# The attention stage of a hybrid decoder layer: another order in the vector engine's step, squares from SBUF, splits one per step, a negated minimum

## The chip, the cores and the metric

The kernel runs on one core of one Trainium2 chip. The metric is the device time of one execution in microseconds (us). The kernel before was run three times, with a median of 1177.88 us (1175.91 to 1178.47).

## The reference

One decoder layer on x (1024 tokens of width 1024), all in float32. What matters here is its differential attention: 4 heads, each with two score matrices from 64-wide queries and keys, one set of 128-wide values, causal, with a slope per head (ALiBi).

```python
def block(qb):
    sc = einsum('bhcqd,bhckd->bhcqk', q_blk, k) * scale          # scale = 64 ** -0.5, c = 0, 1
    bias = where(dist >= 0, -slopes[:, None, None] * dist, -inf)
    prob = softmax(sc + bias[None, :, None], axis=-1)
    att = prob[:, :, 0] - lam * prob[:, :, 1]
    return einsum('bhqk,bhkd->bhqd', att, v)
att = rms_norm(att, head_norm_w, HEAD_NORM_EPS) * (1.0 - lambda_init)
```

Around it stand, in order: RMSNorm and the input projection, a recurrent branch (RG-LRU), the output projection with its residual, and a mixture of 32 experts with a router.

## The kernel before

The program has three blocks, each ended by a barrier of all engines: `project_and_recur`, `attend` and the block that mixes, routes and runs the experts. Only `attend` is touched.

Names used below. TensorE is PE, VectorE is DVE, ScalarE is ACT, GpSimd is POOL and SyncE is SP, as in the profile. Each engine takes its own instructions in the order written, and semaphores order them across engines.

`attend` goes through 4 heads of 8 query tiles of 128 rows. Step s of a head takes the tile with the most keys first: tile s sees 8 - s blocks of 128 keys (`width[s]`), so the tiles become narrower through a head. `pipeline(emit)` runs 32 steps and 4 more that drain. In one step every engine works on several tiles, each a fixed number of steps behind (`behind(h, s, k)`):

- PE: scores of tile s (L687) into the two score buffers `ps_s`, the transposes of tile s-2 (L699) into `ps_t`, the product with the values of tile s-3 (L708) into one of two buffers `ps_o`.
- DVE: for each of the two score matrices, add the bias and keep the row maximum in one instruction (L642, L644, each with a read of its accumulator), then the negated and scaled maximum (L647). Then for tile s-1 the reciprocal of the row sums (L652), a coefficient (L654) and the combination of the two probabilities (L656). Last, for tile s-4, the scaling of the result in `ps_o` by the reciprocal row sum into `mixT` (L665).
- ACT: copy of the transposed tile s-2 (L589), the two exponentials of tile s with their row sums (L594), and for tile s-4 the squares of the result with their sum (L604), read from `ps_o` and scaled there.

Three hand-overs order this. The scores of a step wait for `scores_read`, counted after both DVE instructions of the step before, since there is one pair of score buffers. The exponentials wait for `max_ready`, counted by L647. The product L708 waits until `ps_o` is free, that is for `out_squared` of the tile two before it (s-5), counted by ACT's squares, which come after DVE's scaling of that tile (`out_scaled`).

Once per head the queries and keys of the next head are split into a high part (ACT, L581) and a rest (DVE, L629), one instruction of 128x1024 for each of q and k on each engine. ACT does both in step 2, ahead of the squares; DVE does both in step 4, ahead of L665. PE asks for them (`qk_split`) at the start of the next head, and after the last of them SP issues the load of `w_out` into `qkvT`.

The bias of a head is one tensor `bias8`, 128x1024. POOL multiplies it in place by a constant between two heads (L570), after the last scores of a head were read and before the first of the next.

Of the kernel before, what the change touches and what calls it, by code (L numbers as in the profile page):

```python
# [5 lines left out]
P = 128  # L6
F32 = mybir.dt.float32
# [12 lines left out]
DH = 128  # L20
# [464 lines left out]
def attend(nc, io, persist):  # L485
# [4 lines left out]
    with ExitStack() as ctx:  # L490
# [3 lines left out]
        v_nat = persist["v_nat"]  # L494
        bias8, lam_in = persist["bias8"], persist["lam_in"]
# [4 lines left out]
        row_max = sb("row_max", [P, TT, 2])  # L500
        neg_max = sb("neg_max", [P, TT, 2])
# [9 lines left out]
        lam_exp = sem("lam_exp")  # L511
        pool_own = sem("pool_own")
# [4 lines left out]
        max_ready = sem("max_ready")  # L517
        exp_done = sem("exp_done")
# [42 lines left out]
        @block.gpsimd  # L561
        def _(pool):

            with pool.Fori(1, HEADS) as h:

                pool.wait_ge(scores_read, h * TT + 1)
                pool.sem_inc(pool_own, 1)
                pool.tensor_scalar(bias8[:, :], bias8[:, :], 2.0 ** (-8.0 / HEADS), 1.0,  # L570
                                   ALU.mult, ALU.mult).then_inc(bias_ready, 1)

        @block.scalar
        def _(act):
# [3 lines left out]
            def split(h):  # L578

                for parts, row in ((q_parts, h), (k_parts, h + 4)):  # L580
                    act.activation(part_of(parts, h % 2, 0), tile(qkvT, row), ACT.Copy).then_inc(qk_high, 1)  # L581

            def emit(h, s):
                if at := behind(h, s, 2):
                    n, head, e = at
                    act.wait_ge(turned, n + 1)

                    act.wait_ge(pv_done, n + 1)
                    act.activation(attT[:, e % 2, 0:width[e]], ps_t[:, 0:width[e]], ACT.Copy).then_inc(turned_out, 1)  # L589
                if at := behind(h, s, 0):  # L590
                    n, head, e = at
                    act.wait_ge(max_ready, n + 1)
                    for c in range(2):
                        ins = act.activation(prob[:, e % 4, c, 0:width[e]], prob[:, e % 4, c, 0:width[e]], ACT.Exp,  # L594
                                             bias=neg_max[:, e, c:c + 1], scale=QK ** -0.5,
                                             accum_out=row_sum[:, e, c:c + 1])
                    ins.then_inc(exp_done, 1)
                if s == 2 and not last(h):
                    split(h + 1)
                if at := behind(h, s, 4):  # L600
                    n, head, e = at

                    act.wait_ge(out_scaled, n + 1)
                    act.activation(junk[:, e % 2], ps_o[e % 2][:, 0:DH], ACT.Square, scale=inv_sum[:, e, 0:1],  # L604
                                   accum_out=head_ss[:, span(head * TT + tile_of[e], 1)]).then_inc(out_squared, 1)


            act.sem_inc(qk_high, 2)
            pipeline(emit)

        @block.vector
        def _(dve):
            link = Link(dve, dve_own)
            dve.sem_inc(scores_read, 1)

# [9 lines left out]

            def split(h):
                dve.wait_ge(qk_high, h * 2 + 2)
                for parts, row in ((q_parts, h), (k_parts, h + 4)):
                    dve.tensor_tensor(part_of(parts, h % 2, 1), tile(qkvT, row),  # L629
                                      part_of(parts, h % 2, 0).bitcast(F32), ALU.subtract).then_inc(qk_split, 1)  # L630

            def emit(h, s):
                if at := behind(h, s, 0):
                    n, head, e = at
                    if s == 0:
                        dve.wait_ge(bias_ready, h + 1)

                    dve.wait_ge(scores_done, n + 1)

                    dve.sem_inc(dve_seen, 1)  # L640
                    b = bias8[:, SEQ - width[e]:SEQ]
# [4 lines left out]
                    dve.sem_inc(scores_read, 1)  # L646
# [12 lines left out]
                if s == 4 and not last(h):  # L659
                    split(h + 1)  # L660
                if at := behind(h, s, 4):
                    n, head, e = at
                    dve.wait_ge(pv_done, n + 3)
                    o = mixT[:, span(head + 4, 1), tile_of[e] * P:tile_of[e] * P + P]
                    dve.tensor_scalar(o.rearrange("p o n -> p (o n)"), ps_o[e % 2][:, 0:DH], inv_sum[:, e, 0:1], None,  # L665
                                      ALU.mult).then_inc(out_scaled, 1)

# [3 lines left out]
        def _(pe):  # L671
            for free, n in ((turned_out, 1), (pv_done, 2), (out_squared, 2)):
# [18 lines left out]
            def emit(h, s):  # L691
# [9 lines left out]
                if at := behind(h, s, 3):  # L701
# [3 lines left out]

                    pe.wait_ge(out_squared, n + 1)
                    for k in range(TT - e):
# [1188 lines left out]
```

## Time and profile before

| | us |
|---|---|
| median of 3 runs (lowest, highest) | 1177.88 (1175.91, 1178.47) |
| the profiled execution, its own time | 1176.9 |
| the span that its profile covers | 1174.8 |
| busy in the span: PE, DVE, ACT, POOL | 1056.3, 878.4, 729.8, 130.7 |
| mean granted clock of PE, share of full speed | 0.944 |
| `attend`, first bias addition to end of last scaling | 272.76 to 404.98 |

The profile shows one execution. "Busy" is the time in which an engine had an instruction in its datapath. For a matmul the end is modelled. The granted clock is what the throttle gave PE: 1.00 is 2.4 GHz and 0.50 is 1.2 GHz. A row of the timeline gives start, duration, engine, line, operation, output<-inputs and shape; in brackets stands how long the engine had been idle before it and whose work ended that. PEld is the load of PE's weights, DVEq the instruction queue of DVE (a semaphore step that is an instruction of its own).

### The profile page before, as it was taken

To read this page: it belongs to the slowest core of one execution; us is meant where nothing else is said; L and a number is where in the kernel's file an instruction comes from. 1 tells how busy PE (TensorE), PEld (TensorE's weight loads), DVE (VectorE), ACT (ScalarE), POOL (GpSimd) and SP (SyncE) were. 2 spreads that over 40 slices of the span, in tenths; PEclk is the share of its full clock that TensorE was granted. 3 is DMA by queue.
4 is the path that set the end of the run, shared out by engine and by line. 5 is a ranking of instruction groups with operands and counts; after the bars stand their busy time and mean duration, and the time that the engine had idled before them with its cause. 6 is when DMAs were issued, how large, how long until landed. Compare 5 with 4: busy or idle time off the path is not lost.

```text
span 1174.8 us, 15610 instructions
## 1 busy us (share of the span) xinstructions
PE 1056.3 (90%) x5171; PEld 870.6 (74%) x5171; DVE 878.4 (75%) x1287; ACT 729.8 (62%) x953; POOL 130.7 (11%) x162
## 2 busy tenths in 40 slices
PE   4899999997777799994999999999999999999950
PEld 3788777786565688883888888888888888888830
DVE  6311266505778777768799999999999999999977
ACT  6222465615656832223688888888888888888824
POOL 1000000000000100001021221221221211211110
PEclk7899999998889999995999999999999999999985
DMA  7111111100004164457599999999999999999577
GB/s 230 52 57 50 37 36 36 36 1 0 1 1 146 21 260 139 144 227 259 214 401 389 375 382 389 381 390 385 366 391 376 370 411 367 385 401 377 226 308 286
DMA packets 49526, 273.27 MB, mean 233 GB/s; under 512 B 12016, under 2 KB 22416, under 8 KB 37200
## 3 DMA queue, kind: packets, MB, share of 16 engines
q1 hardware_dynamic: 40144, 255.72, 55.6%
q0 software_dynamic: 9344, 17.06, 3.9%
q8 instruction: 21, 0.34, 0.1%
q14 instruction: 17, 0.14, 0.0%
HBM read 255.97 MB, written 33.55 MB: 246 GB/s over the span
## 4 chain that ended last, share of the span: by engine, by line
PE 59%; DVE 4%; DMA 1%; issue 0%; ACT 0%; SPq 0%; POOL 0%; POOLq 0%; DVEq 0%
PE ps_moe L68 18%; PE ps_moe L70 17%; PE ps_moe L72 17%; PE ps_moe L1382 2%; PE ps_moe L1184 1%; PE ps_moe L1406 1%; DVE qkvT L1777 1%; DVE gate_up L1754 1%; DVE w_lo L1347 1%; DMA y_d<-y_sb,y_entry 1%; DMA y_second<-y_d 1%; PE ps_moe L1174 1%; PE ps_moe L1167 0%; DVE wout_lo L977 0%; PE ps_moe L1234 0%
## 5 line engine op out<-in xcount | busy, mean ns | idle before, releaser
L1347 DVE TENSOR_TENSOR w_lo<-qkvT,w_hi 128x1024 fp32r<-128x1024 f32 x192 | 224.0, 1224 | 3.7 <-ACT w_hi L1343 1.2
L1343 ACT ACTIVATE w_hi<-qkvT 128x1024 fp32r<-128x1024 f32 x192 | 192.7, 1056 | 15.9 <-PE ps_moe L72 15.9
L68 PE MATMUL ps_moe<-w_hi,x_hi 128*128 128x512 f32 x512 | 162.6, 399 | 4.1 <-DVE x_lo L1391 4.1
L70 PE MATMUL ps_moe<-w_lo,x_hi 128*128 128x512 f32 x512 | 159.3, 392 | 0.0
L72 PE MATMUL ps_moe<-w_hi,x_lo 128*128 128x512 f32 x512 | 158.8, 391 | 0.0
L1347 DVE TENSOR_TENSOR w_lo<-gate_up,w_hi 128x1024 fp32r<-128x1024 f32 x128 | 148.1, 1224 | 2.3 <-ACT w_hi L1343 0.4
L1343 ACT ACTIVATE w_hi<-gate_up 128x1024 fp32r<-128x1024 f32 x128 | 126.4, 1056 | 4.9 <-PE ps_moe L72 4.9
L70 PEld LDWEIGHTS ps_moe<-w_lo,x_hi 128*128 128x128 f32 x512 | 96.9, 189 | 20.9
L72 PEld LDWEIGHTS ps_moe<-w_hi,x_lo 128*128 128x128 f32 x512 | 96.7, 189 | 21.0
L68 PEld LDWEIGHTS ps_moe<-w_hi,x_hi 128*128 128x128 f32 x512 | 94.7, 190 | 22.2 <-DVE x_lo L1391 4.5
L333 DVE TENSOR_TENSOR q_parts<-w_raw,k_parts 128x1024 fp32r<-128x1024 f32 x16 | 19.6, 1224 | 91.9 <-ACT k_parts L233 91.9
L68 PE MATMUL ps_moe<-w_hi,h_hi 128*128 128x512 f32 x256 | 82.8, 405 | 5.0 <-DVE h_lo L1415 5.0
L68 PE MATMUL ps_proj<-hT_hi,k_parts 128*128 128x512 f32 x256 | 81.5, 400 | 0.0
L70 PE MATMUL ps_moe<-w_lo,h_hi 128*128 128x512 f32 x256 | 79.8, 393 | 0.0
L70 PE MATMUL ps_proj<-hT_lo,k_parts 128*128 128x512 f32 x256 | 79.7, 393 | 0.0
L72 PE MATMUL ps_moe<-w_hi,h_lo 128*128 128x512 f32 x256 | 79.6, 392 | 0.0
L72 PE MATMUL ps_proj<-hT_hi,q_parts 128*128 128x512 f32 x256 | 79.6, 392 | 0.0
L1361 POOL COPY y_entry<-entries 128x1 int32 (+1 forms) x32 | 32.8, 1025 | 407.9 <-ACT y_sb L1419 407.9
L1347 DVE TENSOR_TENSOR w_lo<-down,w_hi 128x1024 fp32r<-128x1024 f32 x64 | 75.7, 1222 | 0.5
L1343 ACT ACTIVATE w_hi<-down 128x1024 fp32r<-128x1024 f32 x64 | 65.8, 1057 | 7.4 <-PE ps_moe L72 7.4
L1391 DVE TENSOR_TENSOR x_lo<-ps_moe,x_hi 128x1024 fp32r<-128x1024 f32 x32 | 39.2, 1225 | 34.4 <-ACT x_hi L1387 34.4
L1387 ACT ACTIVATE x_hi<-ps_moe 128x1024 fp32r<-128x1024 f32 x32 | 32.8, 1025 | 46.3 <-PE ps_moe L1382 46.3
(255 smaller groups left out, 1880.0 us busy)
## 6 DMA issues: line engine op xcount, KB each, us to landing
qkvT<-in_w_exp_gate SPq DMA_DIRECT2D x16, 2048.0 KB, 10.3
qkvT<-in_w_exp_up SPq DMA_DIRECT2D x16, 2048.0 KB, 15.2
gate_up<-in_w_exp_gate SPq DMA_DIRECT2D x16, 2048.0 KB, 10.6
gate_up<-in_w_exp_up SPq DMA_DIRECT2D x16, 2048.0 KB, 15.4
qkvT<-in_w_exp_down SPq DMA_DIRECT2D x16, 2048.0 KB, 14.5
down<-in_w_exp_down SPq DMA_DIRECT2D x16, 2048.0 KB, 14.7
w_raw<-in_w_in SPq DMA_DIRECT2D x10, 1024.0 KB, 5.2
hn_d<-qkvT SPq DMA_DIRECT2D x16, 512.0 KB, 3.8
```

The lines of the kernel that those rows point to most:

```text
L68: nc_mm(o, lh, rh[h], start=start, stop=False)
L70: nc_mm(o, lh, rl[h], start=False, stop=False)
L72: last = nc_mm(o, ll, rh[h], start=False, stop=stop)
L333: ins = dve.tensor_tensor(w_lo[:, c % 2], w_raw[:, c // 2, :, (c % 2) * P:(c % 2 + 1) * P], w_hi[:, c % 2].bitcast(F32), ALU.subtract)
L1174: mm = pe.transpose(ps_h[:, k // 4, (k % 4) * P:(k % 4 + 1) * P], x2_sb[:, n % 2, k * P:(k + 1) * P], ident[:, :])
L1184: mm = pe.matmul(ps_r[:, AT_LOGITS:AT_LOGITS + NG + NE], x2T[:, n % 2, k], w_rt[:, k], start=k == 0, stop=k == KT - 1)
L1343: act.activation(two(w_hi, r), raw_unit(u, par), ACT.Copy).then_inc(q.split_high, 1)
L1347: dve.tensor_tensor(two(w_lo, r), raw_unit(u, par), two(w_hi, r).bitcast(F32), ALU.subtract).then_inc(q.split_low, 1)
L1361: pool.tensor_copy(copy[:, par:par + 1], entries[:, span(chunk, 1)]).then_inc(ready, 1)
L1382: mm = pe.transpose(ps_t[:, k // 4, (k % 4) * P:(k % 4 + 1) * P], x_sb[:, par, k * P:(k + 1) * P], ident[:, :])
L1387: act.activation(x_hi[:, par], turned_rows(ps_t[:, :, :]), ACT.Copy).then_inc(q.x_high, 1)
L1391: dve.tensor_tensor(x_lo[:, par], turned_rows(ps_t[:, :, :]), x_hi[:, par].bitcast(F32), ALU.subtract).then_inc(q.x_ready, 1)
```

## The change

1. On DVE the scaling of tile s-4 (L665) is the first thing of step s instead of the last.
2. The buffer `ps_o` is free once that scaling is done: PE waits for `out_scaled`. ACT's squares read the scaled result from `mixT` in SBUF, without a scale.
3. The bias additions multiply by -(64 ** -0.5) and keep the minimum, directly into `neg_max`; `row_max`, L647 and `max_ready` go. Each of the two counts `scores_read` when it ends, and each exponential waits for its own of them. The exponential's scale becomes -1.
4. The split of the next head goes one matrix per step: ACT q in step 3 and k in step 4, behind the squares; DVE q in step 4 and k in step 5.
5. Every head has a bias of its own (`bias_more`, 12 KB more per partition). POOL computes the three new ones at the start of `attend`, one from the other, without waiting for scores.

```diff
+        bias_more = sb("bias_more", [P, HEADS - 1, SEQ])
+        bias = [persist["bias8"][:, :]] + [bias_more[:, n] for n in range(HEADS - 1)]
...
-            with pool.Fori(1, HEADS) as h:
-                pool.wait_ge(scores_read, h * TT + 1)
-                pool.sem_inc(pool_own, 1)
-                pool.tensor_scalar(bias8[:, :], bias8[:, :], 2.0 ** (-8.0 / HEADS), 1.0,
+            for h in range(1, HEADS):
+                pool.wait_ge(bias_ready, h)
+                pool.tensor_scalar(bias[h], bias[h - 1], 2.0 ** (-8.0 / HEADS), 1.0,
                                    ALU.mult, ALU.mult).then_inc(bias_ready, 1)
...   (ACT)
-                    act.wait_ge(max_ready, n + 1)
                     for c in range(2):
+                        act.wait_ge(scores_read, 2 * n + c + 3)
                         ins = act.activation(prob[:, e % 4, c, 0:width[e]], prob[:, e % 4, c, 0:width[e]], ACT.Exp,
-                                             bias=neg_max[:, e, c:c + 1], scale=QK ** -0.5,
+                                             bias=neg_max[:, e, c:c + 1], scale=-1.0,
                                              accum_out=row_sum[:, e, c:c + 1])
                     ins.then_inc(exp_done, 1)
-                if s == 2 and not last(h):
-                    split(h + 1)
...
-                    act.wait_ge(out_scaled, n + 1)
-                    act.activation(junk[:, e % 2], ps_o[e % 2][:, 0:DH], ACT.Square, scale=inv_sum[:, e, 0:1],
+                    act.wait_ge(out_scaled, n + 3)
+                    need(act, out_squared, n - 1)
+                    act.activation(junk[:, e % 2], mixT[:, head + 4, tile_of[e] * P:tile_of[e] * P + P], ACT.Square,
                                    accum_out=head_ss[:, span(head * TT + tile_of[e], 1)]).then_inc(out_squared, 1)
+                if s in (3, 4) and not last(h):
+                    split(h + 1, s - 3)
...   (DVE: L665 with its wait moved from the end of emit to its start, then)
-                    dve.tensor_tensor_reduce(prob[:, e % 4, 0, 0:width[e]], ps_s[0][:, 0:width[e]], b, 1.0, -3e38,
-                                             ALU.add, ALU.max, row_max[:, e, 0:1])
-                    link(dve.tensor_tensor_reduce(prob[:, e % 4, 1, 0:width[e]], ps_s[1][:, 0:width[e]], b, 1.0,
-                                                  -3e38, ALU.add, ALU.max, row_max[:, e, 1:2]))
-                    dve.sem_inc(scores_read, 1)
-                    dve.tensor_scalar(neg_max[:, e, :], row_max[:, e, :], -(QK ** -0.5), None,
-                                      ALU.mult).then_inc(max_ready, 1)
+                    for c in range(2):
+                        dve.tensor_tensor_reduce(prob[:, e % 4, c, 0:width[e]], ps_s[c][:, 0:width[e]], b, -(QK ** -0.5),
+                                                 3e38, ALU.add, ALU.min, neg_max[:, e, c:c + 1]).then_inc(scores_read, 1)
...
-                if s == 4 and not last(h):
-                    split(h + 1)
+                if s in (4, 5) and not last(h):
+                    split(h + 1, s - 4)
...   (PE)
-                pe.wait_ge(scores_read, h * TT + (s + 1))
+                pe.wait_ge(scores_read, 2 * (h * TT + s) + 2)
...
-                    pe.wait_ge(out_squared, n + 1)
+                    pe.wait_ge(out_scaled, n + 1)
```

## Rows read from the trace of the kernel before

**Rows 1.** Chain that ended last, its earliest piece that does work (start, us).
```profile
405.75 0.63 ACT c_hi L898
```

**Rows 2.** Windows, by head: length, busy PE, PEld, DVE, ACT, POOL, clock, DMA share, GB/s.
```profile
272.76:305.90 33.14, 25.17 (x167) 20.49 (x168) 24.88 (x67) 20.39 (x48) 1.05 (x1) 0.79 0.00 1
305.90:341.46 35.56, 27.50 (x182) 22.76 (x180) 26.53 (x75) 22.09 (x56) 1.04 (x1) 0.81 0.00 1
341.46:373.75 32.29, 23.22 (x182) 18.37 (x181) 26.49 (x74) 23.12 (x60) 1.04 (x1) 1.00 0.23 78
373.75:404.98 31.23, 25.95 (x183) 20.84 (x181) 25.64 (x79) 22.90 (x64) 0.00 (x0) 0.89 0.14 57
```

**Rows 3.** Waits in 270 to 406: who waited for whom, total us, times, longest.
```profile
DVE prob L642 <- PE ps_s L687: 18.5, 18, 2.7
PE ps_o L708 <- ACT junk L604: 17.4, 15, 2.4
```

**Rows 4.** Windows, one per step of head 2 (steps 0 to 7), cut at L642's starts.
```profile
341.46:345.64 4.18, 2.81 (x21) 1.95 (x19) 3.45 (x10) 2.18 (x6) 0.00 (x0) 1.00 0.00 0
345.64:349.89 4.25, 2.19 (x18) 1.64 (x18) 4.03 (x10) 3.22 (x8) 0.00 (x0) 1.00 0.00 0
349.89:353.73 3.84, 2.69 (x23) 2.12 (x24) 3.62 (x11) 3.40 (x8) 0.00 (x0) 1.00 0.00 0
353.73:359.52 5.79, 3.98 (x31) 3.24 (x32) 3.30 (x11) 5.30 (x13) 0.00 (x0) 1.00 0.00 0
359.52:364.84 5.32, 3.66 (x31) 2.99 (x29) 5.10 (x11) 2.33 (x5) 0.00 (x0) 1.00 0.01 3
364.84:367.88 3.04, 2.32 (x20) 2.10 (x21) 2.50 (x11) 2.65 (x9) 0.00 (x0) 1.00 0.51 131
367.88:370.22 2.34, 2.34 (x22) 1.97 (x21) 2.11 (x9) 1.86 (x7) 0.00 (x0) 1.00 0.94 278
370.22:373.75 3.53, 3.23 (x25) 2.36 (x24) 2.37 (x9) 2.18 (x9) 1.04 (x1) 1.00 1.02 413
```

**Rows 5.** Timeline of head 2, step 0: from the last bias addition on.
```profile
343.75 0.08 DVE L644 DVE_READ_ACCUMULATOR2_ANT row_max<- 128x1 f32 x1
343.95 1.50 PE L687 MATMUL ps_s<-k_parts,q_parts 64*128 64x512 f32 x12 [0.97 <-DVEq L646]
344.06 0.16 DVE L652 RECIPROCAL inv_sum<-row_sum 128x2 f32<-128x2 f32 x1
344.51 0.35 DVE L656 SCALAR_TENSOR_TENSOR prob<-prob,coef 128x128 f32<-128x128 f32 x1
```

**Rows 6.** Timeline, step 3 of heads 1 and 2: first product with the values.
```profile
322.08 2.02 PE L708 MATMUL ps_o<-qkvT,attT 128*128 128x128 f32 x16 [2.26 <-ACT junk L604]
356.41 2.02 PE L708 MATMUL ps_o<-qkvT,attT 128*128 128x128 f32 x16 [1.81 <-ACT junk L604]
```

**Rows 7.** Timeline, steps 4 and 5 of heads 0 to 2.
```profile
296.16 2.77 PE L708 MATMUL ps_o<-qkvT,attT 128*128 128x128 f32 x12 [2.35 <-ACT junk L604]
331.23 2.90 PE L708 MATMUL ps_o<-qkvT,attT 128*128 128x128 f32 x12 [2.35 <-ACT junk L604]
...
363.44 1.22 DVE L629 TENSOR_TENSOR k_parts<-qkvT,k_parts 128x1024 fp32r<-128x1024 f32 x1
364.58 0.34 DVE L665 TENSOR_SCALAR mixT<-ps_o,inv_sum 128x128 f32<-128x128 f32 x1
```

**Rows 8.** Windows of head 1, steps 1 and 5.
```profile
310.10:315.10 5.00, 3.74 (x18) 2.89 (x18) 4.11 (x9) 3.92 (x11) 0.00 (x0) 0.50 0.00 0
330.51:335.26 4.75, 4.03 (x19) 3.61 (x20) 2.50 (x10) 2.81 (x9) 0.00 (x0) 0.50 0.00 0
```

**Rows 9.** Timeline, step 7 of head 0: POOL's bias and DVE beside it.
```profile
303.05 1.05 POOL L570 TENSOR_SCALAR bias<-bias 128x1024 f32<-128x1024 f32 x1 [67.75 <-DVEq L646]
303.22 0.88 DVE L654 SCALAR_TENSOR_TENSOR coef<-row_sum,lam,inv_sum 128x1 f32<-128x1 f32 x1
```

**Rows 10.** Groups of instructions in 270 to 406, the first bias addition.
```profile
L642 DVE CUSTOM_DVE_ANT_0 prob<-ps_s,bias 128x1024 f32<-128x1024 f32 (+7 forms) x32 | 24.2, 756 | 20.6 <-PE ps_s L687 18.5 <-issue 2.0
```

More of the change, by code:

```diff
@@ L494, in attend @@
         v_nat = persist["v_nat"]
-        bias8, lam_in = persist["bias8"], persist["lam_in"]
+        bias_more = sb("bias_more", [P, HEADS - 1, SEQ])
+        bias = [persist["bias8"][:, :]] + [bias_more[:, n] for n in range(HEADS - 1)]
+        lam_in = persist["lam_in"]
         prob = sb("prob", [P, 4, 2, SEQ])
@@ L499, in attend @@
         lam = sb("lam", [P, 8])
-        row_max = sb("row_max", [P, TT, 2])
         neg_max = sb("neg_max", [P, TT, 2])
@@ L511, in attend @@
         lam_exp = sem("lam_exp")
-        pool_own = sem("pool_own")
         qk_high = sem("qk_high")
@@ L516, in attend @@
         scores_read = sem("scores_read")
-        max_ready = sem("max_ready")
         exp_done = sem("exp_done")
@@ L576, in _, with split @@
             act.activation(lam[:, 2:4], lam[:, 0:2], ACT.Exp).then_inc(lam_exp, 1)
-            def split(h):
-                for parts, row in ((q_parts, h), (k_parts, h + 4)):
-                    act.activation(part_of(parts, h % 2, 0), tile(qkvT, row), ACT.Copy).then_inc(qk_high, 1)
+            def split(h, side):
+                parts, row = ((q_parts, h), (k_parts, h + 4))[side]
+                act.activation(part_of(parts, h % 2, 0), tile(qkvT, row), ACT.Copy).then_inc(qk_high, 1)
             def emit(h, s):
@@ L613, in _ @@
             link = Link(dve, dve_own)
-            dve.sem_inc(scores_read, 1)
+            dve.sem_inc(scores_read, 2)
             dve.sem_inc(qk_split, 2)
@@ L624, in _, with split @@
             link(dve.tensor_scalar(lam[:, 5:6], lam[:, 4:5], -LAM_INIT, None, ALU.add))
[L626 to L630, printed above, removed]
-            def emit(h, s):
+            def split(h, side):
+                parts, row = ((q_parts, h), (k_parts, h + 4))[side]
+                dve.wait_ge(qk_high, h * 2 + side + 1)
+                dve.tensor_tensor(part_of(parts, h % 2, 1), tile(qkvT, row),
+                                  part_of(parts, h % 2, 0).bitcast(F32), ALU.subtract).then_inc(qk_split, 1)
+            def emit(h, s):
+                if at := behind(h, s, 4):
+                    n, head, e = at
+                    dve.wait_ge(pv_done, n + 3)
+                    o = mixT[:, span(head + 4, 1), tile_of[e] * P:tile_of[e] * P + P]
+                    dve.tensor_scalar(o.rearrange("p o n -> p (o n)"), ps_o[e % 2][:, 0:DH], inv_sum[:, e, 0:1], None,
+                                      ALU.mult).then_inc(out_scaled, 1)
                 if at := behind(h, s, 0):
@@ L640, in emit @@
                     dve.sem_inc(dve_seen, 1)
-                    b = bias8[:, SEQ - width[e]:SEQ]
-                    dve.tensor_tensor_reduce(prob[:, e % 4, 0, 0:width[e]], ps_s[0][:, 0:width[e]], b, 1.0, -3e38,
-                                             ALU.add, ALU.max, row_max[:, e, 0:1])
-                    link(dve.tensor_tensor_reduce(prob[:, e % 4, 1, 0:width[e]], ps_s[1][:, 0:width[e]], b, 1.0,
-                                                  -3e38, ALU.add, ALU.max, row_max[:, e, 1:2]))
-                    dve.sem_inc(scores_read, 1)
-                    dve.tensor_scalar(neg_max[:, e, :], row_max[:, e, :], -(QK ** -0.5), None,
-                                      ALU.mult).then_inc(max_ready, 1)
+                    b = bias[head][:, SEQ - width[e]:SEQ]
+                    for c in range(2):
+                        dve.tensor_tensor_reduce(prob[:, e % 4, c, 0:width[e]], ps_s[c][:, 0:width[e]], b, -(QK ** -0.5),
+                                                 3e38, ALU.add, ALU.min, neg_max[:, e, c:c + 1]).then_inc(scores_read, 1)
                 if at := behind(h, s, 1):
@@ L658, in emit @@
                                              op0=ALU.mult, op1=ALU.add).then_inc(att_ready, 1)
-                if s == 4 and not last(h):
-                    split(h + 1)
[L661 to L666, printed above, removed]
+                if s in (4, 5) and not last(h):
+                    split(h + 1, s - 4)
             pipeline(emit)
@@ L671, in _ @@
         def _(pe):
-            for free, n in ((turned_out, 1), (pv_done, 2), (out_squared, 2)):
+            for free, n in ((turned_out, 1), (pv_done, 2), (out_scaled, 2)):
                 pe.sem_inc(free, n)
```

## The prediction

> **What bounds the kernel now.** Three views were read, in this order: the chain of waits for where the end is decided, the windows by head and step for who is busy, and the list of waits with the timeline for what each idle stretch waits for. The chain begins with ACT's first work of the last block, at 405.75 us [rows 1]: it cannot be followed through the barrier that ends `attend`. What comes behind is one unbroken chain, so every us by which `attend` ends earlier comes off the end. `attend` itself must be read by its waits.
>
> The four heads take 33.1, 35.6, 32.3 and 31.2 us, and in none is an engine busy throughout: DVE is busy 25 to 27 us, PE 23 to 28, ACT 20 to 23 [rows 2]. So the stage is bound by hand-overs. Head 2, which ran wholly at full clock, shows where: DVE is busy for 4.03 of 4.25 us in step 1 and 3.62 of 3.84 in step 2, so DVE bounds those; in step 3 it is busy for 3.30 of 5.79, in step 4 DVE for 5.10 of 5.32 while PE has 3.66 [rows 4]. The list of waits names the two large ones: DVE waits 18.5 us for scores, PE waits 17.4 us before its product with the values for ACT's squares [rows 3]. They are one wait: PE's queue holds the next scores behind that product.
>
> **The change part by part.**
>
> *The buffer is freed by DVE's scaling, which is first in its step (edits 1 and 2).* In step 3 PE stood still before the first product of heads 1 and 2 for 2.26 and 1.81 us, until ACT's squares ended [rows 6]; ACT had put two splits of a later head ahead of them. The scaling it will wait for is then over a step old. PE goes from transposes to product at once, the scores follow directly, and the interval shrinks by the idle time: -2.26 and -1.81. What is late next is PE itself: 3.98 us busy in that step [rows 4]. For head 3 the same wait was short (I take 0.4, from PE's place in the step), and head 0 had no earlier tiles in step 3. Does the scaling, now ahead of the bias addition, hold it up? It waits for the product of tile s-4, and PE does that before the scores of step s, for which the bias addition waits anyway. A scaling takes 0.34 us [rows 7] and lies beside those scores. Where DVE is bound it costs what it cost at the end of the step. Only the drain gains more: its last three products no longer wait for squares, some 0.3 us less each from the duration of scaling plus squares; I take -0.7 for the drain.
>
> The squares read SBUF. ACT has 9 us idle in every head [rows 2] for eight of them, so each would have to grow by over 1 us to matter: between -0.1 and +0.1 us each, hidden, counted 0. The trace has no square from SBUF; the Trainium skill (ScalarE: Activation LUTs, "The pipeline for one element") says that ScalarE lies closer to PSUM, which speaks against this edit; by it the squares get a little dearer, and the sum stays.
>
> *The split goes one per step (edit 4).* Step 4 holds both of DVE's splits; each takes 1.14 us of its queue (362.31 or so to 363.44 to 364.58) ahead of the scaling [rows 7]. That scaling, and then the squares, are what PE waits 2.35 us for in step 5 of heads 0, 1 and 2 [rows 7]. With one split moved out and the negation gone (below) step 4 becomes 5.32 - 1.14 - 0.23 = 3.95, still DVE's: -1.37 in each of three heads. Step 5 gets the other split: DVE's 2.50 busy [rows 4] less 0.17 for the negation plus 1.14, 3.5 with its gaps, against 3.04 in head 2 (+0.5). In head 1 the step took 4.75 us, because PE began its product late and at half clock, after the idle time [rows 8]; there it is -1.2, and in head 0, whose product took 2.77 instead of about 1.6 [rows 7], about -1.1. ACT's splits, 1.0 us each, stand in steps 3 and 4 behind the squares. Step 3 had 5.30 us of ACT, which includes two splits [rows 4]; with one and without the squares' place in line it has about 4.0 in a step of 4.0, so ACT is close to a bound there. DVE needs q one step later, which leaves about 1.4 us; if ACT slips by more, each us is lost once per head. The load of `w_out`, which SP issues after head 3's last split, moves by under 1 us against its head's start; it was in by step 0 of head 3 (the DMA columns of [rows 2, 4]), a head before it is read.
>
> *Negated minimum (edit 3).* From the end of the last accumulator read (343.83) to L652 are 0.23 us, in which L647 stood; then 0.45 to L656 [rows 5]. The 0.23 goes wherever DVE is the bound: steps 1, 2 of heads 1 to 3 and, counted above, step 4. PE started its scores 0.12 us after that read, through a queue instruction; a count by the instruction itself should take about 0.05, so -0.07 in step 0, where the ring "both additions, scores, both additions" bounds (4.18 us with DVE busy only 3.45 [rows 4]). The exponentials start some 1.5 us earlier, but nobody waited for them: 0 now, slack for ACT above. Steps 6 and 7 together go from 5.87 to about 5.24 in head 2: the additions of tile 6 (0.78), to L656 (0.45), that combination (0.62), the transposes and product behind it (1.5), scores of the next head (1.7) and hand-overs (0.2). That is -0.63, about -0.6 in head 0 and -1.0 in head 1 (low clock).
>
> Does the addition with another scale and a minimum cost more? The trace has only one form, 756 ns in the mean, 32 of them and as many beside it [rows 10]. I take the same: it is one pass over the row either way. The bounds are -0 and, if it took a second pass, twice that; the far end is a rival below.
>
> *A bias per head (edit 5).* Three POOL instructions of 1.05 us move from the head boundaries to the start. At the boundary DVE's coefficient L654 took 0.88 instead of 0.22 us beside L570 [rows 9]; PE had more to do in that step, so nothing is gained. At the start they meet four tiny DVE instructions and perhaps the first bias addition, which had 0.7 us to spare. Bounds: 0, and 3 x 1.05 less 0.7, 2.4. I take +0.4, since a row shows 0.66 for one such meeting and only the last matters. The Trainium skill (SBUF - State Buffer, "Who interferes with whom") has the rule: a DVE instruction with two SBUF inputs and a GpSimd one that reads SBUF exclude each other, while DVE with one SBUF input is not touched. L654 agrees (0.88 us); by it the first bias addition, with one input in PSUM, is not held, and the cost is between 0 and 0.4.
>
> **The sum** against the profiled execution's 1176.9 us, which is 1.0 below the median:
>
> | | removed, us |
> |---|---|
> | head 0 | 1.37 + 1.1 + 0.6 + 0.2 = 3.3 |
> | head 1 | 0.1 + 0.2 + 2.26 + 1.37 + 1.2 + 1.0 = 6.1 |
> | head 2 | 0.07 + 0.2 + 0.2 + 1.81 + 1.37 - 0.5 + 0.63 = 3.8 |
> | head 3 | 0.3 + 0.4 + 0.4 + 0.7 = 1.8 |
> | start | -0.4 |
>
> Together 14.6, so 1162.3: 1162 us. The heads would take about 29.9, 29.4, 28.5 and 29.4 us.
>
> **The rivals.**
>
> *A. PE's clock keeps or takes back part of it.* Heads 0 and 1 ran at 0.79 and 0.81, head 2 at 1.00 [rows 2], and half clock followed PE's idle time: step 5 of head 1 at 0.50 stands behind the 2.35 us [rows 7, 8], step 1 at 0.50 behind the ring of step 0. My sum lets the first kind go, since its idle time goes. For that: the gap is gone. Against: step 1 of head 1 fell without a gap over 2 us. If they stay, heads 0 and 1 lose 1.1, 1.2 and 0.4 + 0.3 again: 1165. If head 2 also gets two such spells (head 1 was 3.3 us longer in all): 1168. The other way round, if the ring's spells vanish too (5.00 against 4.25 in heads 1 and 3, 0.8 each), 1160. The Trainium skill (TensorE: Matmul & The Clock Gate, Part 1) says that the low level is the default and activity lifts it; a fuller PE should then have fewer spells, which is the 1160 end. The trace fits, head 1 apart.
>
> *B. DVE's order is the bound after all.* DVE is busy for 26 us a head; if every gap removed on PE is filled by DVE waiting elsewhere (ACT's slip above, splits arriving late in steps 4 and 5), the two stalls give half: 14.6 less half of 2.26 + 1.81 + 3 x 1.37 + 2.3, 9.4: 1168. For it: steps 1, 2 and 4 are DVE's already. Against: step 3, where the largest stall is, has 2.5 us of DVE idle.
>
> *C. Slower: the new form of the bias addition.* It is on the ring and in DVE's own bound in every step. Its 64 instructions take 48.4 us, twice 24.2 [rows 10]. From +0.23 us each, 30% more, it eats the 14.6; at a second pass the time is 1162 + 48 = 1210. Against it: the addition, the comparison and the multiplication are one instruction already, with a scale of 1.0.
>
> **How the numbers follow.** Forecast, 1158 to 1166: 0.70. A or B beyond it, to 1170: 0.17. More than forecast, below 1158 (the exponentials' head start or a shorter ring give more): 0.08. C or another cost that turns the sign: 0.03. No difference: 0.02. Faster is 0.95, within 0.2% (about 2.4 us, what a measurement of this kernel can tell) 0.02, slower 0.03. The range runs from 1156 to 1168: it takes in A's 1165 and the edge of its 1168, and the start's bounds.
>
> **What would show it.** L708 of step 3 no longer behind ACT's line, with under 0.5 us idle ahead of it; the same in step 5; L647 gone and L652 within 0.1 us of the accumulator read; steps 4 and 5 of heads 0 to 2 near 4.0 and 3.5 us; three L570 in a row near 270 to 274; mean clock of heads 0 and 1 over 0.85. The prediction is wrong if PE's wait before L708 is replaced by one for L589 (ACT), if DVE waits for `qk_high`, if L642 is slower than 756 ns in the mean, or if the heads stay over 31 us.

## The result, and the profile after

The changed kernel takes 1158.62 us in the median of four runs (1158.39 to 1158.93), the one before 1177.81; 19.2 us less. The ratio is 0.9846 (95% interval 0.9832 to 0.9861), which is 16 to 20 us less. Forecast were 1162 and a range of 1156 to 1168.

The profiled execution took 1158.54 us with a span of 1156.7. The last block now begins at 385.67 us instead of 405.73 [rows 1]; behind it lie 771.0 us instead of 769.1. That difference is not the change's: over the profiled executions of the experiments below this part took 768.1 to 771.7 us without relation to the edits. Nor is it the change's that `attend` began 0.55 us earlier, for DVE's first instruction in it did too (269.87 against 270.45 us). `attend` itself, from the first bias addition to the end of the last scaling, fell from 132.22 to 112.75 us: 19.5 us.

The windows by head of the kernel after (stretch, length, busy time of PE, PEld, DVE, ACT, POOL, granted clock, DMA share, GB/s) answer to [rows 2]; the last one ends with the last scaling:

```profile
272.21:301.80 29.59, 23.32 (x167) 19.07 (x168) 23.21 (x60) 19.95 (x48) 0.72 (x1) 0.83 0.01 1
301.80:329.57 27.77, 23.25 (x182) 19.36 (x181) 24.62 (x66) 21.57 (x58) 0.00 (x0) 0.94 0.00 1
329.57:357.72 28.15, 23.38 (x182) 19.42 (x181) 24.55 (x66) 21.60 (x58) 0.00 (x0) 0.94 0.12 34
357.72:384.96 27.24, 22.07 (x183) 18.56 (x181) 24.16 (x70) 21.52 (x64) 0.00 (x0) 1.00 0.31 124
```

The heads became 3.6, 7.8, 4.1 and 4.0 us shorter. DVE's busy time fell by only 1.5 to 1.9 us a head; the rest is idle time that went. DVE is now busy for 87 to 89% of heads 1 to 3, so it is nearly the bound.

The windows by step of head 2 answer to [rows 4]:

```profile
329.57:333.70 4.13, 2.56 (x22) 1.98 (x21) 3.29 (x9) 3.07 (x7) 0.00 (x0) 1.00 0.00 0
333.70:338.08 4.38, 2.73 (x18) 2.08 (x17) 3.95 (x8) 2.74 (x7) 0.00 (x0) 0.78 0.00 0
338.08:341.62 3.54, 3.27 (x23) 2.82 (x23) 3.47 (x8) 1.82 (x3) 0.00 (x0) 0.79 0.01 2
341.62:345.36 3.74, 3.74 (x31) 3.21 (x32) 3.15 (x9) 3.74 (x12) 0.00 (x0) 1.00 0.00 0
345.36:349.24 3.88, 3.88 (x36) 3.51 (x35) 3.81 (x10) 3.88 (x12) 0.00 (x0) 1.00 0.02 6
349.24:352.70 3.46, 2.93 (x27) 2.53 (x26) 3.39 (x10) 3.38 (x9) 0.00 (x0) 1.00 0.00 0
352.70:354.63 1.93, 1.19 (x12) 0.86 (x11) 1.86 (x9) 1.43 (x7) 0.00 (x0) 1.00 0.14 38
354.63:357.72 3.09, 3.09 (x25) 2.43 (x26) 1.64 (x9) 1.55 (x7) 0.00 (x0) 1.00 0.97 275
```

Read the length against each engine's busy time: in step 0 none fills it (the ring of additions and scores, 4.13), in steps 2, 4, 5 and 6 DVE does but for 0.07 us, in steps 3 and 7 PE does. In step 4 PE and ACT are full as well. Step 1 holds a spell at half clock (0.78 in the mean) and is 4.38 us long with DVE busy for 3.95.

The waits between 270 and 388 us answer to [rows 3]. The row for PE's product behind ACT's squares is gone, and that product waits for nothing else; what is left in the main is PE waiting for DVE's additions and DVE for PE's scores, the two sides of the ring:

```profile
PE ps_s L682 <- DVE neg_max L648: 16.6, 13, 2.8
DVE prob L648 <- PE ps_s L682: 13.3, 17, 2.8
ACT junk L601 <- DVE mixT L636: 0.3, 1, 0.3
```

In the timeline of head 2 the first product of step 3 has no idle time in brackets, against 1.81 us [rows 6], the one of step 5 starts at 348.79, 0.45 us before its step begins, and one split stands in each of two steps [rows 7]:

```profile
342.33 1.95 PE L703 MATMUL ps_o<-qkvT,attT 128*128 128x128 f32 x16
...
347.84 1.22 DVE L628 TENSOR_TENSOR q_parts<-qkvT,q_parts 128x1024 fp32r<-128x1024 f32 x1
...
348.79 1.50 PE L703 MATMUL ps_o<-qkvT,attT 128*128 128x128 f32 x12
...
348.98 0.34 DVE L636 TENSOR_SCALAR mixT<-ps_o,inv_sum 128x128 f32<-128x128 f32 x1
...
350.19 0.08 DVE L648 DVE_READ_ACCUMULATOR2_ANT neg_max<- 128x1 f32 x1
350.19 0.16 DVE L653 RECIPROCAL inv_sum<-row_sum 128x2 f32<-128x2 f32 x1
...
351.31 1.22 DVE L628 TENSOR_TENSOR k_parts<-qkvT,k_parts 128x1024 fp32r<-128x1024 f32 x1
```

### The profile page after: what moved, and what is told of

Read it like the earlier page. It is cut to its first block, busy times and chain, and to the rows that moved or that the text cites. A ratio compares the mean times of both kernels' runs of the same rounds, so it can differ in the third digit from the quotient of the medians.

```text
span 1156.7 us, 15563 instructions
## 1 busy us (share of the span) xinstructions
PE 1049.0 (91%) x5171; PEld 866.5 (75%) x5171; DVE 872.4 (75%) x1255; ACT 726.7 (63%) x953; POOL 130.5 (11%) x162
## 4 chain that ended last, share of the span: by engine, by line
PE 60%; DVE 4%; DMA 1%; issue 1%; ACT 0%; SPq 0%; POOL 0%; POOLq 0%; DVEq 0%
PE ps_moe L68 18%; PE ps_moe L70 18%; PE ps_moe L72 18%; PE ps_moe L1377 2%; PE ps_moe L1179 1%; PE ps_moe L1401 1%; DVE qkvT L1772 1%; DVE gate_up L1749 1%; DMA y_d<-y_sb,y_entry 1%; DVE w_lo L1342 1%; DMA y_second<-y_d 1%; PE ps_moe L1169 1%; PE ps_moe L1162 0%; DVE wout_lo L972 0%; PE ps_moe L1229 0%
## 5 line engine op out<-in xcount | busy, mean ns | idle before, releaser
L1382 ACT ACTIVATE x_hi<-ps_moe 128x1024 fp32r<-128x1024 f32 x32 | 32.8, 1026 | 46.2 <-PE ps_moe L1377 46.2
```

The source lines that it names most:

```text
L1382: act.activation(x_hi[:, par], turned_rows(ps_t[:, :, :]), ACT.Copy).then_inc(q.x_high, 1)
```

## The experiments

Each is timed in five rounds, beside runs of the kernel before, whose median was 1176.4 to 1178.4 us. The last block alone differs by up to 3.6 us from one profile to the next, so a second measure stands beside the medians: the length of `attend` itself in the one profiled execution of each run, first bias addition to end of last scaling.

| run | median, us | `attend`, us |
|---|---|---|
| kernel before | 1177.8 | 132.22 |
| before, edit 2 alone | 1165.5 | 118.57 |
| before, edit 4 alone | 1168.9 | 123.81 |
| before, edits 2 and 4 | 1163.6 | 118.18 |
| changed kernel | 1158.6 | 112.75 |
| changed, edit 4 undone | 1160.2 | 115.90 |
| changed, PE waits for the squares | 1160.4 | 113.38 |
| changed, edit 1 undone | 1158.8 | 113.42 |
| changed, edit 3 undone | 1162.9 | 118.00 |
| changed, edit 5 undone | 1158.0 | 112.38 |
| changed, scores of step 1 by matrix | 1152.6 | 107.95 |
| changed, product ahead of transposes | 1158.7 | 115.13 |
| changed, DVE's other order | 1155.8 | 110.16 |
| changed, both of the improvements | 1150.2 | 103.98 |

"Theory S" is the prediction's: two stalls of PE, both behind squares that stand behind splits, and DVE's own work for the rest.

### One part alone, on the kernel before

**Edit 2 alone.** PE takes the buffer after the scaling; ACT's squares read `mixT`, as in the change (not repeated here); nothing else.

```diff
-            for free, n in ((turned_out, 1), (pv_done, 2), (out_squared, 2)):
+            for free, n in ((turned_out, 1), (pv_done, 2), (out_scaled, 2)):
...
-                    pe.wait_ge(out_squared, n + 1)
+                    pe.wait_ge(out_scaled, n + 1)
```

> The kernel before with edit 2 alone: PE takes the values' buffer when the scaling is done, the squares read the scaled result; the order, both splits in one step and the separate negation stay. Theory S (two stalls, both PE waiting for squares that stand behind splits): the 2.26, 1.81 and 0.4 us ahead of the first product in step 3 go; the 2.35 us in step 5 shrink only by a square (0.5), because the scaling itself stands behind both DVE splits; the drain gives 1. Together 6 to 7 us less, 1171. Rival F (freeing by the scaling is nearly the whole change): 1162 or less. Rival O (DVE's work alone sets the time, waits are hidden): no difference.

Measured: 1165.49 us (1161.13 to 1167.38), ratio 0.9899 (0.9883 to 0.9916), 11.6 us less. The mechanism is S's, the size is not. Steps 3 to 5 of head 2, as windows:

```profile
346.94:350.67 3.73, 3.73 (x31) 3.20 (x32) 3.29 (x11) 3.73 (x8) 0.00 (x0) 1.00 0.00 0
350.67:355.99 5.32, 3.66 (x31) 2.98 (x29) 5.10 (x11) 3.57 (x11) 0.00 (x0) 1.00 0.00 2
355.99:358.62 2.63, 2.25 (x19) 1.95 (x20) 2.41 (x10) 2.24 (x7) 0.00 (x0) 1.00 0.38 97
```

Step 3 lost its stall (5.79 to 3.73), step 4 with both DVE splits is still 5.32 [rows 4]. In step 5 the product still waits 1.85 us, now for the scaling behind the splits. What S left out is the clock: steps 1 and 5 of head 1, at 0.50 before [rows 8], take 4.24 and 2.63 us here, against 4.25 and 2.63 in head 2.

S also left out a third group of waits, in step 1. Before the change the product of step 1 waited 1.26, 1.35 and 1.36 us for squares in heads 1 to 3, which is 4.0 of the 17.4 us of [rows 3]; behind it PE fell to half clock in heads 1 and 3. With edit 2 alone this wait is gone, and step 1 runs at full clock in heads 1 to 3. It isn't that PE idles less: in steps 0 and 1 of head 1 together it now stands still for 1.64 and 1.71 us around its scores, before for 1.63 and 1.26. Step 1 of head 1, first before and then with edit 2:

```profile
311.49 1.19 PE L708 MATMUL ps_o<-qkvT,attT 128*128 128x128 f32 x4 [1.26 <-ACT junk L604]
312.62 2.29 PE L687 MATMUL ps_s<-k_parts,q_parts 64*128 64x512 f32 x12
```

```profile
309.42 0.61 PE L709 MATMUL ps_o<-qkvT,attT 128*128 128x128 f32 x4
311.74 1.31 PE L688 MATMUL ps_s<-k_parts,q_parts 64*128 64x512 f32 x12 [1.71 <-DVEq L647]
```

**Edit 4 alone.** One split per step, behind the squares.

```diff
-                if s == 2 and not last(h):
-                    split(h + 1)
...   (behind the squares)
+                if s in (3, 4) and not last(h):
+                    split(h + 1, s - 3)
...   (DVE)
-                if s == 4 and not last(h):
-                    split(h + 1)
+                if s in (4, 5) and not last(h):
+                    split(h + 1, s - 4)
```

> The kernel before with edit 4 alone: ACT splits q in step 3 and k in step 4 behind the squares, DVE q in step 4 and k in step 5. Theory S: the squares of step 2 are no longer behind two splits, so step 3 loses its stall (4 to 4.5 us in all); step 4 loses 1.14 three times, step 5 gains 1.14 of DVE but loses most of the 2.35 us wait. Together 8 to 10 us less, 1169. Rival F: under 3 us less, because PE still waits for squares. Rival O: no difference.

Measured: 1168.86 us, ratio 0.9932 (0.9919 to 0.9945), 8.3 us less, where S had it. Steps 1 and 3 to 5 of head 1:

```profile
306.94:311.95 5.01, 3.68 (x19) 2.90 (x18) 4.12 (x10) 3.92 (x11) 0.00 (x0) 0.55 0.01 3
...
315.80:320.14 4.34, 3.97 (x31) 3.23 (x32) 3.30 (x10) 4.32 (x12) 0.00 (x0) 1.00 0.00 0
320.14:324.32 4.18, 3.67 (x31) 2.99 (x29) 3.96 (x10) 2.94 (x6) 0.00 (x0) 1.00 0.00 0
324.32:328.09 3.77, 2.71 (x22) 2.25 (x22) 3.55 (x11) 3.19 (x8) 0.00 (x0) 1.00 0.00 0
```

Steps 3, 4 and 5 fell from 6.24, 5.32 and 4.75. Step 5 runs at full clock; the idle time in it is about half of the 2.35 us before:

```profile
325.04 1.58 PE L708 MATMUL ps_o<-qkvT,attT 128*128 128x128 f32 x12 [1.21 <-ACT junk L602]
```

In step 1, where the wait for squares stays (1.33 us in head 1), PE fell to half clock as before. It still waited 12.8 us in all for squares.

**Edits 2 and 4 together**, both diffs above.

> The kernel before with edits 2 and 4 together. Alone they took 11.6 and 8.3 us. Theory S, as it stands after those runs: both remove the same stall (PE behind squares behind splits), and once the scaling frees the buffer DVE's two splits only move work between steps 4 and 5 (7.95 us together in the run with edit 2 alone, 4.2 + 3.8 with both): 1164 to 1166, no gain over edit 2 alone. Rival P (the splits' place has a gain of its own): 1160 or less.

Measured: 1163.60 us (1161.45 to 1165.25), ratio 0.9892 (0.9877 to 0.9908). Alone they took 11.6 and 8.3 us, together 12.8 (13.7, 8.4 and 14.0 in `attend`): for the most part they remove the same stall. Steps 4 and 5 of head 2 are 7.95 us together, exactly as with edit 2 alone (5.32 + 2.63):

```profile
347.12:351.30 4.18, 3.65 (x31) 2.98 (x29) 3.96 (x10) 3.28 (x8) 0.00 (x0) 1.00 0.03 6
351.30:355.07 3.77, 2.78 (x22) 2.25 (x22) 3.55 (x11) 3.13 (x8) 0.00 (x0) 1.00 0.00 0
```

### One part undone, on the kernel after

**Both splits in one step again** (edit 4 reversed).

```diff
-                if s in (4, 5) and not last(h):
-                    split(h + 1, s - 4)
+                if s == 4 and not last(h):
+                    split(h + 1)
```

and on ACT likewise, back into step 2 ahead of the squares.

> The changed kernel with edit 4 undone: both splits in one step again, ACT's in step 2 ahead of the squares, DVE's in step 4. Theory S: with the scaling first nobody waits for the squares, so DVE's two splits only move work between steps 4 and 5, whose sum is DVE's either way (7.3 us a head): 1 to 3 us over the changed kernel, 1160 to 1162. Rival P (the placement of the splits is the gain whatever frees the buffer): 6 us or more over it, 1165.

Measured: 1160.21 us (1158.32 to 1166.32), ratio 0.9865 (0.9843 to 0.9887). The medians put it 1.6 us over the changed kernel and `attend` 3.2; rival P's 1165 lies just beyond the interval. Steps 4 and 5 of head 1:

```profile
317.88:323.15 5.27, 5.13 (x43) 4.58 (x43) 5.03 (x11) 4.72 (x14) 0.00 (x0) 1.00 0.00 0
323.15:325.48 2.33, 0.74 (x7) 0.54 (x8) 2.26 (x9) 1.60 (x6) 0.00 (x0) 1.00 0.00 0
```

PE did 5.13 us of work in step 4 and 0.74 in step 5 (3.66 and 4.03 before): it runs ahead while DVE splits, and catches nothing up later. The sum, 7.60, is DVE's either way (7.34 after the change). Head 2 did worse in this profile: its step 6 held a spell at half clock and took 3.93 us, against 2.32 in head 1.

**PE waits for the squares again** (the hand-over of edit 2 reversed; the squares still read `mixT`).

```diff
                     pe.wait_ge(out_scaled, n + 1)
+                    pe.wait_ge(out_squared, n + 1)
```

> The changed kernel with PE waiting for the squares again before it takes the values' buffer (they still read the scaled result). Theory S: with the splits behind the squares and the exponentials 1.2 us earlier, ACT has the squares done within 0.3 us of when PE asks; 0 to 2 us over the changed kernel, 1159 to 1161. Rival F: the stalls come back, 6 us or more over it, 1165.

Measured: 1160.36 us, ratio 0.9855 (0.9841 to 0.9869). Rival F falls: with edits 1, 3 and 4 in place the squares are done when PE asks. PE's whole wait for them is this row of its list of waits:

```profile
PE ps_o L704 <- ACT junk L601: 0.5, 2, 0.3
```

So in the changed kernel the hand-over of edit 2 is worth little more. That doesn't make edit 4 its equal: alone on the kernel before it left 12.8 us of waits for squares. What brought them from 12.8 to 0.5 must lie in the other edits, above all edit 1 (the scaling first) or edit 3 (exponentials earlier); neither was undone in this kernel, so which one it is stays open.

**The scaling last in DVE's step** (edit 1 reversed: the block with L636 stands behind the splits).

```diff
-                if at := behind(h, s, 4):      (L636, first in emit)
...
+                if at := behind(h, s, 4):      (L636, last in emit)
```

> The changed kernel with edit 1 undone: DVE scales tile s-4 last in step s again. Theory S: PE then waits for a scaling behind a split in step 5, up to 0.5 us a head, and where scores are the bound the 0.26 us was hidden anyway: 0 to 2 us over the changed kernel, 1159 to 1161. Rival Q (the order is what frees PE early): 4 us or more over it.

Measured: 1158.81 us, ratio 0.9843 (0.9829 to 0.9856): no difference from the changed kernel. The order of edit 1 is worth nothing measurable as long as the scaling frees the buffer; PE waited 3.8 us in all for scalings, the longest 0.75 in step 6.

**Maximum and negation back** (edit 3 reversed).

```diff
-                    for c in range(2):
-                        dve.tensor_tensor_reduce(..., b, -(QK ** -0.5), 3e38, ALU.add, ALU.min,
-                                                 neg_max[:, e, c:c + 1]).then_inc(scores_read, 1)
+                    (two additions with 1.0, -3e38, ALU.max into row_max, the second waited for)
+                    dve.sem_inc(scores_read, 1)
+                    dve.tensor_scalar(neg_max[:, e, :], row_max[:, e, :], -(QK ** -0.5), None,
+                                      ALU.mult).then_inc(max_ready, 1)
```

> The changed kernel with edit 3 undone: maximum, then a separate negation (L647 of the kernel before), one count for both additions, exponentials behind the negation. Theory D (DVE is now the bound in 6 of 8 steps, and each pays the 0.23 us between the last accumulator read and the reciprocal): 32 x 0.23 less the ring's steps, 5 to 7 us over the changed kernel, 1164 to 1166. Rival H (hidden, as PE's queue decides): under 2 us.

Measured: 1162.92 us, ratio 0.9886 (0.9871 to 0.9902), 4.3 us over the changed kernel by the medians and 5.3 by `attend`: at the lower end of theory D's 5 to 7, far over H's 2. Steps 4 to 6 of head 1 are 4.18, 3.78 and 2.23 against 3.88, 3.46 and 1.93: 0.3 us each, not 0.23:

```profile
319.72:323.90 4.18, 4.15 (x37) 3.71 (x36) 3.96 (x10) 4.18 (x11) 0.00 (x0) 1.00 0.00 0
323.90:327.68 3.78, 2.73 (x25) 2.34 (x24) 3.56 (x12) 3.08 (x9) 0.00 (x0) 1.00 0.00 0
327.68:329.91 2.23, 1.18 (x12) 0.85 (x11) 2.01 (x11) 1.14 (x6) 0.00 (x0) 1.00 0.00 0
```

**One bias again, in place** (edit 5 reversed).

```diff
-                pool.wait_ge(bias_ready, h)
+                pool.wait_ge(scores_read, 2 * h * TT + 2)
```

with `bias` four times the same tensor.

> The changed kernel with edit 5 undone: one bias, multiplied in place between two heads. Theory S: at the head boundary DVE's coefficient is held 0.66 us and the first addition waits for POOL, in a step where PE has more to do; at the start DVE meets no POOL work, but had slack there: within 1 us of the changed kernel, 1158 to 1159.5. Rival B (PE's queue has no slack left in step 7): 3 x 0.7 to 3 x 1.5, 2 to 4.5 us over it.

Measured: 1157.99 us, ratio 0.9839 (0.9825 to 0.9852): no difference. Between heads 1 and 2 DVE's coefficient took 1.02 us beside POOL, in step 7, where PE sets the length:

```profile
327.96 1.02 DVE L654 SCALAR_TENSOR_TENSOR coef<-row_sum,lam,inv_sum 128x1 f32<-128x1 f32 x1
...
330.42 1.23 DVE L647 CUSTOM_DVE_ANT_0 prob<-ps_s,bias 128x1024 f32<-128x1024 f32 x1 [0.65 <-issue]
```

### What bounds the changed kernel

**The ring in step 0.** The scores of step 1 go by matrix.

```diff
+                for pair in ((0,), (1,)) if s == 1 else ((0, 1),):
+                    pe.wait_ge(scores_read, 2 * (h * TT + s) + pair[-1] + 1)
...                  (the same matmuls, for c in pair)
+                    mm.then_inc(scores_done, len(pair))
...   (DVE, ahead of each addition)
+                        dve.wait_ge(scores_done, 2 * n + c + 1)
```

> The changed kernel, and in step 1 of each head PE does the scores of the two matrices one after the other, each once its own bias addition of step 0 has read its buffer; DVE waits for each by itself. Theory R (step 0 is bound by the ring both additions, scores, both additions: 4.13 us with DVE busy for 3.3): the step becomes DVE's, 3.4, 0.7 less in four heads, and PE's idle time of over 2 us there shrinks, which spares spells at half clock: 3 to 5 us under the changed kernel, 1154 to 1156. Rival W (matmuls of the two row groups overlap when they alternate, 12 in 1.5 us against 0.21 each; apart they take longer and eat the gain): no difference or up to 1 us over.

Measured: 1152.62 us (1149.81 to 1155.62), ratio 0.9795 (0.9773 to 0.9817), 6 us under the changed kernel by the medians. `attend` became 4.8 us shorter, which is theory R's 3 to 5; the rest of the 6 lies outside the part that was edited. Steps 0 and 1 of head 2, and PE's scores in the timeline:

```profile
326.79:330.06 3.27, 2.98 (x18) 2.49 (x19) 3.20 (x8) 2.39 (x4) 0.00 (x0) 1.00 0.00 0
330.06:334.00 3.94, 2.80 (x22) 2.02 (x21) 3.87 (x10) 3.31 (x11) 0.00 (x0) 1.00 0.00 0
```

```profile
328.08 2.63 PE L683 MATMUL ps_s<-k_parts,q_parts 64*128 64x512 f32 x12 [0.29 <-DVE neg_max L648]
```

The twelve matmuls take 2.63 us apart and 1.50 alternating [rows 5], yet start 1.1 us earlier: rival W's price is real and lies beside DVE's work. 0.86 us in step 0 of each of heads 1 to 3 is 2.6 us. Head 0 gave 1.1, and steps 1 and 2 of heads 1 and 2 another 0.7: these heads run at 1.00 throughout, where the changed kernel had spells at half clock.

**PE's product ahead of its transposes.** The two blocks of PE's `emit` change places.

```diff
-                if at := behind(h, s, 2):      (transposes, ahead of the product)
...
+                if at := behind(h, s, 2):      (transposes, behind it)
```

> The changed kernel with PE's product of tile s-3 ahead of its transposes of tile s-2. Theory: PE's waits for DVE's combination (3.9 us in all, mostly steps 4 to 7) are filled by the product, step 7 gains 0.3: 1 to 2 us under the changed kernel, 1157. Rival: transposes end 0.5 to 2 us later, ACT copies later, the exponentials of tile 3 come after DVE asks for them, and steps 3 and 4 get longer: 1 to 3 us over it.

Measured: 1158.68 us, ratio 0.9851 (0.9833 to 0.9868): no difference by the medians. Both the theory's gain and the rival's cost happened: step 7 is shorter (2.91 against 3.09 in head 2), step 4 longer (4.17 against 3.88). In `attend` the rival wins, 2.4 us over, of which 1.7 lie in the last step and the drain (5.77 against 4.04), which neither had named.

**DVE does not wait for its own results.** Order: first addition, reciprocal, second addition, coefficient, scaling, combination.

```diff
+                        if c == 0:
+                            inverse(h, s)             (wait for exp_done, L653, counted only)
...
+                    dve.wait_ge(dve_own, link.n)
+                    counted(coefficient)
+                    (scaling of tile s-4)
+                    dve.wait_ge(dve_own, link.n)
+                    (combination)
```

> The changed kernel with DVE's step in another order: first addition, reciprocal, second addition, coefficient, scaling of tile s-4, combination, so that no instruction waits for the one before it. Theory D (DVE bounds 5 of 8 steps, and the 0.45 us from the last addition to the combination is mostly waiting for its own results): 0.3 less in some 20 steps, 4 to 6 us under the changed kernel, 1153 to 1155. Rival: the scaling behind the additions holds the buffer and PE waits for it, or PE becomes the bound at once: under 1 us.

Measured: 1155.75 us (1153.67 to 1158.04), ratio 0.9821 (0.9801 to 0.984), 2.9 us under the changed kernel, between theory and rival. Steps 4, 5 and 7 of head 1:

```profile
315.63:319.24 3.61, 3.61 (x33) 3.24 (x32) 3.61 (x10) 3.61 (x9) 0.00 (x0) 1.00 0.00 0
319.24:322.44 3.20, 2.86 (x27) 2.54 (x27) 3.20 (x10) 3.05 (x9) 0.00 (x0) 1.00 0.00 0
...
324.11:327.45 3.34, 3.20 (x25) 2.54 (x26) 1.35 (x9) 1.73 (x9) 0.00 (x0) 1.00 0.02 5
```

Steps 4 and 5 lost 0.27 and 0.26 and DVE is busy throughout both; steps 3 and 7, PE's, took 0.26 and 0.25 back.

**Both improvements.**

> The changed kernel with both improvements: scores of step 1 by matrix, and DVE's step without waits for its own results. They shorten different steps (0 the one; 1, 4 and 5 the other), so they should add: 1158.6 less 6.0 less 2.9, 1149.7, range 1147 to 1152. Rival (PE's queue, already the bound in steps 3 and 7, takes the second gain): 1152 to 1153, no better than the first alone.

Measured: 1150.22 us (1149.99 to 1152.09), ratio 0.9768 (0.9753 to 0.9784). They add: 8.4 us under the changed kernel (8.8 in `attend`, where they gave 4.8 and 2.6 alone) and 27.6 under the one before; step 0 of head 2 is 3.01 us, step 4 3.61:

```profile
326.65:329.66 3.01, 2.72 (x16) 2.30 (x17) 3.01 (x9) 2.13 (x4) 0.00 (x0) 1.00 0.00 0
...
340.45:344.06 3.61, 3.61 (x32) 3.24 (x33) 3.61 (x10) 3.61 (x11) 0.00 (x0) 1.00 0.02 7
```

## Why the prediction was right, and where its sizes were off

**The stall in step 3** was as forecast: edit 2 alone takes it from 5.79 to 3.73, the changed kernel to 3.74 (forecast 3.98) and, in head 1, from 6.24 to 3.60. PE is what is late next, busy 3.74 of 3.74.

**Steps 4 and 5** were forecast at 3.95 and 3.5 and are 3.88 and 3.46. ACT did not become a bound, though it is busy 3.88 of 3.88 in step 4: with DVE's other order that step fell to 3.61.

The prediction booked the two stalls to edits 2 and 4 as if they were separate. The experiments say that this attribution is wrong though the sum is right: 11.6 and 8.3 us alone, 12.8 together, about 2 by the medians when either is undone. In step 5 the stall was one wait for squares behind a scaling behind splits. Neither edit alone ends it: of 2.35 us edit 2 leaves 1.85 and edit 4 leaves 1.21; the changed kernel has none. What the sum gave to moving one split in head 2 is therefore not that edit's own: steps 4 and 5 take 8.36 us before [rows 4] and 7.95 with edit 2 alone, and 7.95 again with edit 4 added.

**The negation** was sized at 0.23 us in DVE's steps; undone it costs 0.3 a step in steps 4 to 6, and 4.3 us in all by the medians, 5.3 in `attend`. Part of it shows in the timeline above: without the negation's wait L653 starts at 350.19 together with the accumulator's read ahead of it, while the negation before began after that read had ended [rows 5]. The read's 0.08 us thus goes as well.

**The scaling first and the bias per head** were taken as 0 and +0.4 (the start). Both undone change nothing clear of noise. The start cost nothing: from DVE's first instruction in `attend` to the first bias addition are 2.34 us, against 2.31 before. There POOL's three instructions met the small ones of DVE:

```profile
269.63 1.05 POOL L568 TENSOR_SCALAR bias_more<-bias 128x1024 f32<-128x1024 f32 x1 [34.89 <-POOLq L82]
269.87 0.87 DVE L618 CUSTOM_DVE_ANT_0 lam_in<-lam_in 128x64 f32<-128x64 f32 x1 [18.90 <-PEq L82]
270.76 2.18 POOL L568 TENSOR_SCALAR bias_more<-bias_more 128x1024 f32<-128x1024 f32 x2
271.17 0.64 DVE L622 TENSOR_TENSOR lam<-lam 128x1 f32<-128x1 f32 x1 [0.27 <-ACT lam L574]
272.21 1.23 DVE L648 CUSTOM_DVE_ANT_0 prob<-ps_s,bias 128x1024 f32<-128x1024 f32 x1 [0.22 <-DVE lam L623]
```

L618 took 0.87 instead of 0.23 us and L622 0.64 instead of 0.16, while the first bias addition started beside a running L568 and took its usual 1.23. The Trainium skill (SBUF - State Buffer, "Who interferes with whom") says that a DVE instruction with two SBUF inputs and a GpSimd one that reads SBUF exclude each other, and one SBUF input is not touched; the trace agrees on both.

**The squares from SBUF** were feared to be a little dearer. They take 302 ns in the mean against 360 from PSUM with a scale. The edit changed two things at once, the place and the scale, which was one value per row. Copies of ACT in the last block of the same profile, without such a scale, show the place by itself: 128x1024 read from PSUM (`ps_moe`) takes 1026 ns, from SBUF (`qkvT`) 1057.

```profile
L1382 ACT ACTIVATE x_hi<-ps_moe 128x1024 fp32r<-128x1024 f32 x32 | 32.8, 1026 | 46.2 <-PE ps_moe L1377 46.2
L1338 ACT ACTIVATE w_hi<-qkvT 128x1024 fp32r<-128x1024 f32 x192 | 192.8, 1057 | 16.7 <-PE ps_moe L72 16.7
```

So SBUF is the slightly dearer source, and the 58 ns that a square saved point to the scale; no run took the two apart on the squares themselves. The Trainium skill's page ScalarE: Activation LUTs ("Step-by-step: what each stage is for") puts ScalarE closer to PSUM, of the place that it writes to; the copies show the same sign for the place that it reads.

**The terms that were mis-sized** are the clock in step 1 and the drain, 2.7 of the 4.9 us by which `attend` beat the sum (19.5 against 14.6). Step 1 of heads 1 and 3, at half clock before, was left at 5.0 us in the sum and came to 4.00 and 3.95, 2.1 us. The prediction put that spell down to the ring of step 0, which the change hardly touches, and did not see the product's wait for squares in step 1 (1.26 us in head 1). In both profiles in which that wait stands, the kernel before and edit 4 alone, step 1 of heads 1 and 3 takes 5.00 to 5.03 us; in the other twelve no step 1 of heads 1 to 3 takes more than 4.60. So the long spells went wherever that wait went. In its size this is the far end of rival A, which got too little weight; why the clock follows that wait is not shown. The drain was taken as -0.7 and gave -1.3 (5.35 to 4.04 from the last step of head 3 on): in the drain before, three of its last four products began after a wait for squares (0.29, 0.41 and 0.28 us), and the exponentials now start earlier there. Step 3 gave 0.2 to 0.4 more than its idle time in each of heads 1 to 3, 0.9 in all, and the start did not cost its 0.4.

One sign of the prediction did not come: head 0 has a mean clock of 0.83, not over 0.85; head 1 has 0.94. The total fell within the range though the sum held these terms at nothing or too small; that much is owed to the width of the range and not to the mechanism.

Rival B (half) and C (a slower addition) fell: the addition takes 754 ns in the mean, 756 before [rows 10].

What stays open is why a spell comes where it comes. Edit 2 alone leaves 1.85 us of PE idle in step 5, and head 0 falls behind it (its step 6 at 0.69) while heads 1 and 2 do not; before, 2.35 us were followed by half clock in heads 0 and 1 and not in head 2. The wait in step 1 was as long in head 2 as in head 3 (1.35 and 1.36), and head 2 did not fall. The changed kernel keeps head 0's spell (steps 0 to 2) and two short ones in heads 1 and 2. The Trainium skill (TensorE: Matmul & The Clock Gate, Part 1) has activity lift the low level; that `attend` as a whole is fuller (PE busy 82% against 77%) and has fewer spells agrees. Head by head it does not show: before the change the head with none was the least full (head 2, 72%).

## What to carry to other kernels

- When a stall is a chain of waits (product behind squares behind scaling behind splits), price the chain, not the edits: two edits that each cut it do not add (11.6 and 8.3 us alone, 12.8 together). Go through every instance of the wait, too; here the third group was the one left out.
- Once the waits are gone, look in the steps for the one in which no engine is full: that is a ring through one buffer pair, and splitting the hand-over by buffer paid here (4.8 us of `attend`, 6 by the medians) even at a price on the engine that had slack.
- Idle time on PE can cost more than itself: behind the same 2.35 us, step 5 took 3.04 us at full clock in head 2 and 4.75 at half in head 1. Bound the forecast by a sum with the spells and one without, and don't put the central value near the first.
- Where an edit touches one block of three, compare that block in the profiles beside the whole time; here the last block moved by up to 3.6 us though nobody edited it, more than several of the edits did.

## What the hardware showed that was not expected

Twelve score matmuls on 64 rows took 1.50 us when they alternated between the two row halves and 2.63 us when each half went alone, at full clock both times. On DVE, a reciprocal, a coefficient and the combination that needs it, each waiting for the one before, took 0.45 us from the start of the first to the start of the last; with other work between them step 4 lost 0.27 of it.
